# Entry of the two expert mixtures of a decoder trunk: routing by halves of the tokens, the rows' low parts on GpSimd, the rank behind the selection, the shared up product in the next group

## The reference

```python
s = sigmoid(t @ router_w)                       # 256 x 64
choice = s + router_bias
gscore = sum(top_k(choice in 8 groups, 2))      # the best 4 groups stay
eidx = top_k(where(emask, choice, -inf), 6)     # 6 experts for each token
w = s[eidx] / sum(s[eidx]) * 2.5                # the gates
routed = sum over 64 experts of (silu(t @ wg) * (t @ wu)) @ wd * gate
shared = (silu(t @ sh_w_gate) * (t @ sh_w_up)) @ sh_w_down
out = routed + shared
```

## Time and profile before

| what | value |
|---|---|
| runs | 1239.65, 1240.75, 1242.38 us; median 1240.75 |
| the profiled execution | 1241.0 us, first to last instruction |
| busy: PE, PEld, DVE, ACT, POOL | 86%, 52%, 33%, 21%, 6% of the span |
| transfers | 447.62 MB, 361 GB/s over the span |
| chain that ended last | PE 52%, DMA 39%, SP's queue 3%, DVE 2% |
| expert stage of layer 0, of layer 1 | about 150 to 600 us, about 777 to 1234 us |
| 620 to 700 us (mixer of layer 1) | 173 GB/s |

### The profile page before, as it was taken

One profiled execution on the slowest core, in us unless ns is written; L12 is line 12 of the kernel. 1 busy time (PEld: TensorE's weight loads), 2 busy tenths in 40 slices (PEclk: granted clock), 3 DMA queues, 4 the chain that ended last, 5 costly groups with the idle time before them and its releaser, 6 DMA issues.

```text
span 1241.0 us, 19501 instructions
## 1 busy us (share of the span) xinstructions
PE 1068.5 (86%) x7694; PEld 647.8 (52%) x7694; DVE 415.0 (33%) x995; ACT 260.3 (21%) x622; POOL 78.7 (6%) x109
## 2 busy tenths in 40 slices
PE   8999998879897986677899999988799788886775
PEld 5784755353535454344688847554445353543442
DVE  3893623222413132221333327232233231322213
ACT  4381411111111111011132223211112111111110
POOL 3064000000000000000340000000000000000000
PEclk9999998989999999798999999999899899989888
DMA  9274799999999999999990545999999999999995
GB/s 346 71 285 190 288 403 413 422 421 412 420 421 421 421 420 420 421 420 416 345 338 35 207 200 237 372 420 421 421 401 421 422 420 422 421 420 421 420 420 212
DMA packets 83450, 447.62 MB, mean 361 GB/s; under 512 B 7822, under 2 KB 25293, under 8 KB 35740
## 3 DMA queue, kind: packets, MB, share of 16 engines
q1 hardware_dynamic: 80870, 439.25, 87.0%
q0 software_dynamic: 2064, 6.98, 1.6%
q10 hardware_dynamic: 422, 0.08, 0.0%
HBM read 445.20 MB, written 1.05 MB: 360 GB/s over the span
## 4 chain that ended last, share of the span: by engine, by line
PE 52%; DMA 39%; SPq 3%; DVE 2%; issue 2%; ACT 1%; POOL 0%; DVEq 0%
DMA ring<-in_l_exp_w_up 22%; DMA ring<-in_l_exp_w_down 15%; PE bank L1168 11%; PE bank L1326 7%; PE bank L1003 5%; PE bank L1361 4%; PE bank L931 4%; PE bank L1006 2%; PE bank L874 2%; DMA ring<-in_l_exp_w_gate 2%; PE bank L1074 2%; SPq L670 2%; PE bank L1131 2%; SPq L732 2%; PE bank L1295 1%
## 5 line engine op out<-in xcount | busy, mean ns | idle before, releaser
L1326 PE MATMUL bank<-ring,big 128*32 128x256 f32 x2816 | 186.2, 425 | 66.6 <-DMA ring<-in_l_exp_w_up 40.8
L1326 PEld LDWEIGHTS bank<-ring,big 128*32 128x32 f32 x2816 | 113.0, 122 | 135.9 <-issue 102.5
L1168 PE MATMUL bank<-ring,big 128*64 128x512 f32 x608 | 149.6, 626 | 23.7 <-DMA ring<-in_l_exp_w_up 23.7
L1168 PEld LDWEIGHTS bank<-ring,big 128*64 128x64 f32 x608 | 49.1, 144 | 114.1 <-issue 113.3
L1361 PE MATMUL bank<-ring,big 128*32 128x512 f32 (+1 forms) x736 | 89.6, 629 | 20.3 <-DMA ring<-in_l_exp_w_down 18.4
L1623 ACT ACTIVATE ys_high<-bank,gcol 128x512 fp32r<-128x512 f32 (+1 forms) x86 | 58.3, 678 | 160.1 <-PE bank L1361 102.8
L2216 DVE TENSOR_TENSOR mixT<-mixT,bank 128x512 f32<-128x512 f32 x120 | 79.9, 685 | 27.1 <-PE bank L1295 17.9
L2186 DVE TENSOR_TENSOR big<-big,bank 128x256 f32<-128x256 f32 x22 | 9.3, 421 | 222.4 <-PE bank L1326 222.4
L1206 PE MATMUL bank<-pick,xs_high 128*128 128x128 f32 x352 | 83.1, 279 | 0.0
L1206 PE MATMUL bank<-pick,xs_low 128*128 128x128 f32 x352 | 81.4, 275 | 0.0
L2351 POOL TENSOR_TENSOR rstd<-rstd,half 128x1 f32<-128x1 f32 x10 | 10.5, 1046 | 1087.2 <-DVE rstd L1726 1087.1
(11 more groups left out here) (308 smaller groups left out, 1422.1 us busy)
## 6 DMA issues: line engine op xcount, KB each, us to landing
ring<-in_l_exp_w_gate SPq DMA_DIRECT2D x122, 1024.0 KB, 13.4
ring<-in_l_exp_w_up SPq DMA_DIRECT2D x122, 1024.0 KB, 17.8
ring<-in_l_exp_w_down SPq DMA_DIRECT2D x114, 1024.0 KB, 17.7
ring<-in_l_w_in SPq DMA_DIRECT2D x13, 1024.0 KB, 12.2
ring<-in_l_w_out SPq DMA_DIRECT2D x8, 1024.0 KB, 8.5
lead_par<-in_l_exp_w_down SPq DMA_DIRECT2D x4, 1024.0 KB, 11.7
ring<-in_l_exp_w_gate SPq DMA_DIRECT2D x8, 512.0 KB, 9.2
ring<-in_l_exp_w_up SPq DMA_DIRECT2D x8, 512.0 KB, 10.8
```

What stands on the lines that cost most here:

```text
L1168: ins = mm(ps[SLOTS * q:SLOTS * q + SLOTS, :], xg[:, c, SLOTS * j:SLOTS * j + SLOTS], both[:, c, 0:n:n - 1], start=(c == 0), stop=(c == C ...
L1326: ins = mm(ps[r, 0:HID], xn[:, c, r], loop_weights(L, j, w)[:, c, :], start=(c == 0), stop=(c == C - 1))
```

## The change

- The router of each half is a product of its own (`route(tb)`), right behind that half's transposes, into a bank of its own; ScalarE takes each half's sigmoid right behind that half's high part; VectorE's selection is written for one half and runs twice (`scores(tb)`, `groups_and_experts(tb)`), with the last copy into `xT` between the scores and the groups of half 0.
- The subtraction that makes `xs_low` moves from VectorE to GpSimd (`low_parts`), behind GpSimd's powers.
- `taken` is counted by half. The rank key and the ranks come right behind the slots; the gates come behind VectorE's copies of gathered pieces. `ranked` moves from the first `gate_up` into the gathers, behind the fifth of eight; `ordered` stands behind VectorE's copy of the sixth piece. VectorE copies pieces 3, 5 and 7, ScalarE the other five (four each before).
- The shared gate products of both halves go to one bank (`sgate`), with one Silu, which moves from the first group into the second. All shared up products (`shared_up`) are made at once with 256 columns behind the gate product of the second group, into another bank (`sup`). SyncE's waits and GpSimd's wait ahead of layer 1's router weights follow them.

```diff
-AHEAD = 5
+AHEAD = 4
+RANKED_BEHIND = 4
+DVE_FIRST = (3, 5, 7)
...
-                sp.wait_ge(S("shared_gates"), L + 1)
+                bank_read(sp, ("sgate", L))
                 into_place(experts, GE - 1, 0)
...
-                bank_read(sp, ("sgu", L, 1))
+                first.read(sp, "sup")
                 into_place(experts, GE - 1, 2)
...
+                def shared_up(lp):
+
+                    unit_wait(pe, ("shared", L, 1))
+                    w = by_chunk(unit(("shared", L, 1)))
+                    ps = lp.open(pe, "sup")
+                    for m in range(2):
+                        for c in range(C):
+                            ins = mm(ps[:, T * m:T * m + T], w[:, c, P * m:P * m + P], xT[:, c, :],
+                                     start=(c == 0), stop=(c == C - 1))
+                    lp.made(ins, "sup")
...
                 xt(1 + 2 * L, 0)
+                pe.wait_ge(S("router_w"), 32 * (L + 1))
+                route(0)
+                shared_gate(0, 0)
                 xt(1 + 2 * L, 1)
...
+                shared_gate(0, 1, 0, AHEAD)
+                route(1)
+                shared_gate(0, 1, AHEAD)
+                shared_gate(1, 0)
+                shared_gate(1, 1, 0, AHEAD)
                 positions()
-                shared_gate_up(0, 1, 1, 0, AHEAD)
+                shared_gate(1, 1, AHEAD)
...
-                        if lp.kind == "first" and pr == 0 and c == 1:
-                            ranked(lp)
...
                             bank_made(gather(c, bank_open(pe, ("gather", L, c))), ("gather", L, c))
+                            if c == RANKED_BEHIND:
+                                ranked(lp)
                         gate_up(lp, 0)
-                        shared_gate_up(0, 1, 1, AHEAD)
+                        pe.wait_ge(lp.sem("pick"), lp.count(2, 2, 0))
...
                         if key == "gate" and behind and behind.kind == "first":
-                            shared_gate_up(1, 0, 1)
-                            shared_gate_up(1, 1, 1)
+                            shared_up(behind)
...
-                for k in range(2):
-                    xt(1 + 2 * L, k)
                 for tb in range(TB):
+                    for k in ((0, 1), (2,))[tb]:
+                        xt(1 + 2 * L, k)
                     act.wait_ge(S("ln_done"), 4 * L + tb + 1)
                     fn(by_piece(xs[0], tb), by_row(xrow, tb), ACT.Copy).then_inc(S("xs_high"), 1)
-                xt(1 + 2 * L, 2)
-                ps = bank_read(act, ("router", L))
-                bank_done(fn(sco, ps[:, 0:TB * NE].rearrange("p (a e) -> p a e", a=TB), ACT.Sigmoid), ("router", L))
+                    ps = bank_read(act, ("router", L, tb))
+                    bank_done(fn(sco[:, tb, :], ps[:, 0:NE], ACT.Sigmoid), ("router", L, tb))
...
+                scores(0)
+                xt(1 + 2 * L, (3,))
+                groups_and_experts(0)
+                scores(1)
+                groups_and_experts(1)
                 ps = bank_read(dve, ("pos", L))
...
                 def first_gathered():

-                    gates_and_ranks()
+                    rank_keys()
+                    ranks()
+                    for c in DVE_FIRST:
+                        gathered(bank_read, bank_done, ("gather", L, c))
+                        if c == RANKED_BEHIND + 1:
+                            ordered(first)
+                    gate_values()
                     link(v.memset(st[:], 0.0))
...
+            def low_parts(L):
+
+                for tb in range(TB):
+                    pool.wait_ge(S("xs_high"), 2 * L + tb + 1)
+                    g.tensor_tensor(by_piece(xs[1], tb), by_row(xrow, tb), by_piece(xs[0], tb), ALU.subtract)\
+                     .then_inc(S("xs"), 1)
```

More of the change, by code:

```diff
@@ L193, in plan_banks @@
         xt(1 + 2 * L)
-        u.add(("router", L), 4)
-        for tb in range(2):
-            u.add(("sgu", L, tb), (1, 7)[tb])
+        for tb in range(TB):
+            u.add(("router", L, tb), 4 + tb)
+        u.add(("sgate", L), 7)
         u.add(("pos", L), 0)
@@ L217, in plan_banks @@
                 seq = [("ranked", 2)] + seq + [("rowsT", 6), ("sorted", 4)]
-            seq = seq + (gather if after == "wide" else pair) + (scatter if form == "wide" else rows)
+            seq = seq + (gather if after == "wide" else pair) + [("sup", 6)] * (kind == "first") + (scatter if form == "wide" else rows)
             u.loop((L, kind), seq, times, but=("pair", "scatter") if kind == "narrow" else ())
@@ L1684, in narrow @@
                         high(lp, key, 0, a, b)
-                for c in range(0, C, 2):
-                    gathered(bank_read, bank_done, ("gather", L, c))
+                for c in range(C):
+                    if c not in DVE_FIRST:
+                        gathered(bank_read, bank_done, ("gather", L, c))
                 alone_groups(L, wide, narrow)
@@ L1989, in prog_vector, with scores @@
-                v.memset(chx[:, :, NE:], SENT)
-                v.memset(want[:], SENT)
-                link(v.tensor_tensor(cho, sco, rbias[:].unsqueeze(1).to_broadcast([P, TB, NE]), ALU.add))
-                for tb in range(TB):
+                def scores(tb):
+                    bank_moved(dve, ("router", L, tb))
+                    if tb == 0:
+                        dve.wait_ge(S("router_w"), 32 * (L + 1))
+                        v.memset(gsx[:], SENT)
+                        v.memset(chx[:, :, NE:], SENT)
+                        v.memset(want[:], SENT)
+                    link(v.tensor_tensor(cho[:, tb, :], sco[:, tb, :], rbias[:], ALU.add))
@@ L2182, in narrow @@
                     elif behind.kind == "first":
-                        shared_hidden(1)
+                        shared_hidden(behind)
                     ps = lp.read(dve, "up")
@@ L2434, in prog_gpsimd @@
             add_bias(1)
-            bank_moved(pool, ("sgu", 0, 1))
+            ExpertLoop(0, "first", banks, S, bank, i=0).moved(pool, "sup")
             router(1)
-            for _ in range(2):
-                for tb in range(TB):
-                    power(rstd[:, tb:tb + 1])
+            for tb in range(TB):
+                power(rstd[:, tb:tb + 1])
+            low_parts(1)
+            for tb in range(TB):
+                power(rstd[:, tb:tb + 1])
         with nc.Block() as block:
```

136 lines of the change are left out of this document (53 added, 83 removed).

## The result

The changed kernel takes 1247.2 us (median of 5 runs), the kernel before 1240.75 beside it. The ratio on record is 1.0044, with a 95% interval of 1.0031 to 1.0056; the two medians alone give 1.0052. I had forecast 1241.9, no difference that can be measured. It is slower. The median lies 0.7 us above the end of my range; 1.0044 times 1240.75 is 1246.2, just inside it.

What follows compares the result with a forecast made beforehand. Bound by the expert weight stream at about 420 GB/s, which gains only from an earlier start or fewer gaps. Layer 0 at -0.05 and layer 1 at -0.85 made 0.9 us slower than 1241.0: 1241.9 us, range 1234.0 to 1246.5.

Steps and rivals of the forecast that it cites:

- Part 4: Low-part subtraction on GpSimd: 2.7 us, holding VectorE's selection chain for its length less 0.3; g -1.65 and -1.95.
- g: How much earlier "taken" of the second half comes, in us; forecast -1.65 in layer 0, -1.95 in layer 1.
- the prediction's sum: Per layer 1.1 + g, plus 0.5 in layer 0: -0.05 and -0.85, together 0.9 us slower.
- one 32-column row: VectorE instruction of 32 columns took 0.98, not 0.19, beside a 2.76 us GpSimd one; taken as a shorter hold.
- Part 1: Rank right behind the selection, gates later: slots to order 4.1 us instead of 6.67, order 2.55 + g earlier.
- Part 3: Entry, routing by halves without the move to GpSimd: "taken" in layer 0 at 136.7, g = +1.87.
- Part 2: Shared up products out of the entry: TensorE's second product 0.85 + g earlier; no gap at 202, layer 0 gains 0.5.
- (b): Slower by the clock: gathers and first gate/up product at half clock, about 3 us; one layer 1244.9, both 1247.9; chance 0.20.
- What the stream keeps: Stream behind the entry: each layer keeps the smaller of 2.55 + g and 0.85 + 0.25 + g, 1.1 + g.
- the pair of 173.00: Weight transfers issued at 173.00 in layer 0, waiting for TensorE, 2.0 us before the stream ran dry; 1.75 needed to issue.
- (a): GpSimd and VectorE hardly meet: g = +1.87, 6.4 us gained in all, 1234.6; chance 0.26.
- (c): The pair of 173.00 holds the stream less: each layer keeps 1.25 more, 1239.4 with blocked chains; chance 0.12.

Runs made afterwards that it cites:

- g3: The kernel before with the two low-part subtractions moved to GpSimd and nothing else; 1255.9 us, ratio 1.0078 to 1.0118.
- h1: The changed kernel with GpSimd's low-part subtraction replaced by a one-input multiplication by zero; 1245.5 us, ratio 1.0010 to 1.0030.
- h3: The changed kernel with sixteen shared gate products repeated ahead of the second half's transposes; 1251.1 us, ratio 1.0059 to 1.0090.
- i1: The changed kernel with the selection chain's 4 and 6 column copies written as a multiplication by one; 1247.1 us, ratio 1.0028 to 1.0063.
- f2: The changed kernel with GpSimd waiting for both halves to be normalised before its first low part; 1247.3 us, ratio 1.0021 to 1.0057.
- f3: The changed kernel without the low-part subtractions, products reading the high parts twice (other numbers result); 1237.3 us, ratio 0.9946 to 0.9981.
- f1: The changed kernel with both low-part subtractions back on VectorE; 1246.8 us, ratio 1.0020 to 1.0052.
- f4: The changed kernel with routing in one block and low parts on VectorE as before, keeping early rank and moved up products; 1241.9 us.
- g2: The kernel before with only the shared up products moved to the next group; 1242.5 us, ratio 0.9989 to 1.0012.
- h2: f4 with eight shared gate products repeated while TensorE waits for the selection; 1241.0 us, ratio 0.9981 to 1.0006.
- g1: The kernel before with only the rank moved right behind the selection; 1243.0 us, ratio 0.9995 to 1.0017.

## Why the prediction was wrong, step by step

**Part 4 failed, first of all in one clause of it:** "the low part of half 0 cannot start before 128.45 (VectorE's last normalising instruction has the port)". Both instructions follow GpSimd's power, so they start together: VectorE's 0.02 ahead in layer 0 (where GpSimd's also needs ScalarE's high part, done 0.04 us behind the power), GpSimd's 0.12 ahead in layer 1 (756.64). VectorE's was the one that stood still, in both layers of all five kernels that let them race (changed, g3, h1, h3, i1). So not a 0.2 us bias add was held but the instruction on which TensorE, and then everything, waits. g came to -3.17 and -3.87, I had -1.65 and -1.95; the two misses add up to 3.4 us of the 3.6 by which the profiled total was off (1245.5 against 1241.9). With the measured g the prediction's sum gives 1.6 slower in layer 0 and 2.8 in layer 1, together 4.3; measured 2.4 and 2.1, together 4.5. That the sum fits better than its parts is luck.

The length of the hold was the second error. I had discounted the rule of the Trainium skill (SBUF — State Buffer, Who interferes with whom) on the strength of one 32-column row. The copy held 2.81 of 2.84, the bias add of f2 2.79. The rule's whole instruction was right for the two-input form, and so is its list: a plain copy and a tensor_scalar can take the shared pair too, which I had read over, counting only two-input instructions. The 2.84 itself was near the 2.7 taken.

Run f2 shows that the clause alone would not have saved the forecast. It makes the assumed order true, and its g is -2.5 and -1.6, for which the prediction's sum gives 1.4 us slower. It is 4.8 us slower (1.0039 of before). The held chain leaves TensorE idle, and the clock falls in both layers; the sum had nothing for that. So in the changed kernel the hold on the normalising instruction is what happened, but without it the loss would have come by the way of f2.

**Part 1 was right:** slots to order 4.29 (4.1 forecast).

**Part 3 was right only where nobody makes the low parts.** There g = 1.75 (1.87 forecast; f3). It said "without the move to GpSimd", with VectorE's subtractions hidden behind the router as before. Run f1 is that kernel, and its g is -1.4 and -1.8: in halves the subtractions are no longer hidden.

**Part 2 was right in its terms and left one out.** TensorE's second product came at 156.37: 0.85 + g from 154.16 gives 156.48. The gap at 202 went and the wait shrank (in f2, and in layer 1 of h1 and i1, it was 1.1 to 2.7 us again). What its sum left out is the clock behind the idle time in front of the rank counts, 2.3 us in f4 and g2, which rival (b) counted only for long waits ("From about 2.7 us on"). In these entries idle times of 1.96, 2.33 and 2.34 us were followed by the low clock; others of 1.97, 2.34 and 2.90 were not. The idle time alone doesn't decide, and the bound that I drew from two rows was worthless.

**What the stream keeps** came out in f3 only (3.3 and 2.8 for 3.35 and 2.84). For 1.6 and 1.1 f4 kept 0.5 and 0.5, and h2, with the full clock, 0.9 and -1.2; g1 kept -1.6 and 0.4 for 0.25. I had seen that the pair of 173.00 waits for TensorE; that the eight halves do too was hidden, since the order was the later of the two before.

**Rivals.** (a) needs low parts that hold nobody; f3, without them, took 1237.3 for its 1234.6. (b) gave nearly the right time, 1247.9 for both layers, but not by its own mechanism: gathers and first product ran at full clock in the changed kernel, and i1 shows nearly the same delay without the low clock. That the range reached up to the result was thus luck too, since its upper end came from (b). Gathers at half clock are real in f1, g2 and h3, and in one layer each of f2, f4 and h1; f4 prices them at 1.2 us, not 3. (c) is out: f4 kept 0.5 in each layer where (c) asked for 2.35 and more.

Open: why GpSimd's instruction goes first in these near ties; why the stream keeps so little of an earlier order and second product in h2; and what decides the gap that each layer has some 165 us behind the entry, between 0.5 and 3.4 us of stream in these executions, by which it can hide or feign a microsecond of any edit.

## What to carry to other kernels

Before an elementwise instruction is moved from VectorE to GpSimd, look at what VectorE runs in the same microseconds: beside a two-input GpSimd instruction its two-input instructions, its copies from SBUF and its tensor_scalars stood still here, so for these the pair is one engine, and GpSimd is the slower half of it (2.84 against 2.12 us for this subtraction). If the moved instruction is released together with VectorE's critical one, count on losing the race. Cutting a chain in halves doubles its small instructions and takes away the wait in which other work was hidden (f1): price the halves with that work in them. And work that leaves a waiting stage takes its cover along: TensorE's filler went, 2.3 us of idling remained, and in some of the entries the clock fell with it.

## What the hardware did that I had not expected

- A subtraction on GpSimd that starts 0.02 us behind a VectorE instruction of 1.29 us holds it for 2.65; a start 0.02 us ahead is no protection. (The Trainium skill, in the section named above, gives the pair to whoever issues first; the start times of layer 0 say the other.) With 0.05 us (the penalty add at 764.38) and 0.15 us (the bias add in layer 1 of f2) VectorE's instruction went through at its usual time.
- A copy of six columns can take 2.81 us, while a maximum and a copy out of PSUM beside the same kind of subtraction keep their 0.23 and 0.69.
- One-input work of the same size on GpSimd is slower than two-input work (3.78 against 2.84 us) and holds VectorE for 1.7 to 1.9 us, not for its length.
- With 2.33 and 2.34 us of idling in front of the same products, TensorE's granted clock fell to 0.50 once and stayed at 1.00 once; with 2.90 us it fell in h3 and stayed in i1.
